# Weight slots at 0, 128 and 256 bytes modulo 512, and activation groups each at its own place, in a two-block transformer kernel

## The chip, the cores and the metric

The kernel runs on one core of one Trainium2 chip. The metric is the device time of one execution in microseconds. Three executions of the kernel before took 3440.49, 3443.15 and 3453.31 us; their median is 3443.15 us. The profiled execution is a separate one.

## The reference, cut to what matters

The input is one sequence of 512 tokens with 1024 features, all in float32. Two layers of a first block come first, each with a SwiGLU feed-forward part (1024 to 2816 and back), a token mixer (an attention with compressed, selected and windowed branches, beside a latent attention) and a second SwiGLU part. A hybrid layer follows, with an mLSTM, a forgetting attention, a gated linear recurrence, a gated linear attention, and a feed-forward part of 4096.

```python
for l in range(DEPTH):                       # DEPTH = 2
    mod = c_act @ w_ada[l] + b_ada[l]
    x = x + 0.5 * g1 * swiglu(modulate(x, sh1, sc1), ffn1_gate[l], ffn1_up[l], ffn1_down[l])
    x = x + g2 * token_mix(modulate(x, sh2, sc2), ...)
    x = x + 0.5 * g3 * swiglu(modulate(x, sh3, sc3), ffn2_gate[l], ffn2_up[l], ffn2_down[l])
x = rms_norm(x) * final_norm
...
z = h @ w_in + b_in                          # second block
merged = jnp.sum(g * yb, axis=2)
x = x + merged @ w_o
x = x + jnp.square(jax.nn.relu(h2 @ w_up)) @ w_down
```

Nearly all of the arithmetic is in products of an activation matrix with a weight matrix. The rest is small.

## The kernel before, in words

Activations stay in SBUF with features on the partitions, as tiles of 128 partitions by 512 tokens. Weights stream from HBM in a fixed order, written out by `plan()`: each step of it is one block of up to 1024 float32 per partition, loaded by SyncE into one of five `raw` buffers.

**Products in three parts.** Each large product is computed from operands that are split into a high and a low part, both in the type float32r. A weight block is split by ScalarE (line 971: `wh` is the rounded copy of `raw`) and VectorE (line 1492: `wl = raw - wh`), two steps of the plan ahead of TensorE. There are three slots (`NW = 3`), so `wh0` to `wh2` and `wl0` to `wl2`, used in turn by the split blocks. An activation is split in the same way into pairs such as `uh` and `ul`. TensorE then runs three matmuls for each 128 by 128 piece of weights (`three`, lines 451 to 453), with the weights as the stationary operand and the 512 tokens as the moving one:

```python
TE.matmul(o, w_hi(i, k), h, start=first, stop=False)
TE.matmul(o, w_lo(i, k), h, start=False, stop=False)
return TE.matmul(o, w_hi(i, k), l, start=False, stop=last)
```

`fm` (a whole product column), `fm_pair` (two of them interleaved) and the gate pieces during attention call it. Lines 538 to 540 are the same three for the first weights of the kernel. In `tm` (lines 485 to 487) the activations are stationary, in pieces of 128 tokens, and the weights move: 512 columns wide, or 280 wide for `inT` (three pieces of 280 columns in one slot, so they begin 0, 1120 and 2240 bytes after its start).

**Other matmuls** are plain float32: scores (673), transposes (568), attention times values (690, 696), sums over partitions (494, 512, 516), rows of norms (501), and filler matmuls (506).

**Order.** Each engine's program is written out by hand, and semaphores alone order the engines among each other. No wait hangs on where a tile lies. Addresses come from the order in which the tiles are declared: `sb()` puts each behind the one before it, at a multiple of 32 bytes, and tiles declared in a `with` block give their room to the next block.

**Places before.** All places here are bytes of one partition, modulo 512. The first tile, `cst`, begins at 128 and is 4764 bytes long, so `x` begins at 288; every tile between it and `mod` is a multiple of 512 bytes long. So `x`, `raw`, all `wh` and `wl`, `uh`, `ul`, `acc` and `tmp` begin at 288. The tiles `level` (64 bytes, after `mod` and `small`) and `level_mix` (384 bytes) hold no data and bring what follows to 288 again: `fh`, `fl`, `oA`, `oB`, `mq`, `mk`, `kk`, `vt`, `qh`, `ql`, `ch`, `cl`, `mP`, `mT`, `slope`, `oAh`, `oAl`, `oBh`, `oBl`, `merged`, `bh`, `bl` and `sg`. Exceptions are `mmask` and `mv` (416), `pcT` and `vc` (160), and the tiles of the second block's branches (`lqk` 416, `lE` 480). Pieces of a weight block follow each other in steps of 512 bytes, and the activation pieces in steps of 2048 bytes. So every float32r matmul but those 280 wide begins both of its reads at the same place modulo 512. The tables `ones`, `ident` and `sel` in `cst` are at 284.

Of the kernel before, what the change touches and what calls it, by code (L numbers as in the profile page):

```python
# [5 lines left out]
NW = 3  # L6
# [238 lines left out]
def program(nc, A, OUT):  # L245
# [3 lines left out]
    F32, F32R = mybir.dt.float32, mybir.dt.float32r  # L249
# [13 lines left out]
    top = ExitStack()  # L263

    def sb(ctx, name, shape, dt=F32):
        return ctx.enter_context(nc.sbuf_tensor(f"s_{name}", shape, dt))
# [2 lines left out]
    cst = sb(top, "cst", [128, ncol])  # L269
    x = sb(top, "x", [128, 8, 512])  # L270
    raw = [sb(top, f"raw{i}", [128, 1024]) for i in range(NRAW)]
    wh = [sb(top, f"wh{i}", [128, 1024], F32R) for i in range(NW)]
    wl = [sb(top, f"wl{i}", [128, 1024], F32R) for i in range(NW)]
    uh = sb(top, "uh", [128, 8, 512], F32R)
    ul = sb(top, "ul", [128, 8, 512], F32R)
    acc = sb(top, "acc", [128, 512])
# [3 lines left out]
    sb(top, "level", [128, 16])  # L280

    with ExitStack() as c:
        fh = sb(c, "fh", [128, CHUNK_FF, 512], F32R)
        fl = sb(c, "fl", [128, CHUNK_FF, 512], F32R)
        crow = sb(c, "crow", [128, 1024])
        more = sb(c, "more", [128, 512])
    with ExitStack() as c:
        fsq = sb(c, "fsq", [128, 8, 512])
    with ExitStack() as c:
        oA, oB = sb(c, "oA", [128, 4, 512]), sb(c, "oB", [128, 4, 512])  # L290
        mq = sb(c, "mq", [128, 8, 512])
        mk = sb(c, "mk", [128, 8, 512])
        with ExitStack() as c1:
            kk = sb(c1, "kk", [128, 2, 512])
            vt = sb(c1, "vt", [128, 4, 256])
            gt = sb(c1, "gt", [128, 4, 24])
            pcT = sb(c1, "pcT", [128, 4, 2, 128])
            vc = sb(c1, "vc", [128, 4, 128])
            kc = sb(c1, "kc", [128, 64])
            mmask = sb(c1, "mmask", [128, 512])  # L300
            mv = sb(c1, "mv", [128, 4, 512])
            sb(c1, "level_mix", [128, 96])
            with ExitStack() as c2:
                qh, ql = sb(c2, "qh", [128, 3, 512], F32R), sb(c2, "ql", [128, 3, 512], F32R)
                ch, cl = sb(c2, "ch", [128, 2, 512], F32R), sb(c2, "cl", [128, 2, 512], F32R)
            with ExitStack() as c2:
                dist = sb(c2, "dist", [128, 512])
                slope = [sb(c2, f"slope{i}", [128, 512]) for i in range(2)] + [tmp[2], tmp[3]]
                mP = [sb(c2, f"mP{i}", [128, 512]) for i in range(4)] + [tmp[0], tmp[1]]
                mT = [sb(c2, f"mT{i}", [128, 512]) for i in range(3)] + [acc]  # L310
                mfew = sb(c2, "mfew", [128, 24])
        oAh, oAl = sb(c, "oAh", [128, 4, 512], F32R), sb(c, "oAl", [128, 4, 512], F32R)
        oBh, oBl = sb(c, "oBh", [128, 4, 512], F32R), sb(c, "oBl", [128, 4, 512], F32R)
    with ExitStack() as c:
        merged = sb(c, "merged", [128, 8, 512])
        bh, bl = sb(c, "bh", [128, 4, 512], F32R), sb(c, "bl", [128, 4, 512], F32R)
        sg = sb(c, "sg", [128, 8, 512])
        bgh = sb(c, "bgh", [128, 32])
        ffx = sb(c, "ffx", [128, 512])
        rows = sb(c, "rows", [128, 512])  # L320
        with ExitStack() as d:
            lqk = sb(d, "lqk", [128, 8, 512])
            lmo = sb(d, "lmo", [128, 4, 512])
            lai, lmx = (sb(d, n, [4, 512]) for n in ("lai", "lmx"))
            lfm = sb(d, "lfm", [36, 512])[32:36, :]
            lsum = sb(d, "lsum", [128, 384])
            lcol = sb(d, "lcol", [128, 4, 4])
            lv = sb(d, "lv", [128, 4, 512])
            lE = [sb(d, f"lE{i}", [128, 512]) for i in range(4)]
        with ExitStack() as d:  # L330
            xqk = sb(d, "xqk", [128, 8, 512])
            xcol = sb(d, "xcol", [128, 4, 4])
            xgs = sb(d, "xgs", [128, 1])
            xsq = sb(d, "xsq", [128, 8, 512])
            xv = sb(d, "xv", [128, 4, 512])
            xP = [ffx] + [sb(d, f"xP{i}", [128, 512]) for i in range(3)]
            xT = [xsq[:, 5 + i, :] for i in range(3)]
            xfew = sb(d, "xfew", [128, 24])
        with ExitStack() as d:
            rbd = sb(d, "rbd", [128, 1024])  # L340
            rsp, rs1 = sb(d, "rsp", [128, 4]), sb(d, "rs1", [128, 4])
            rhb = sb(d, "rhb", [128, 12])
            rxc = sb(d, "rxc", [128, 4, 512])
            rR, rI, rT = (sb(d, n, [128, 4, 512]) for n in ("rR", "rI", "rT"))
            rgy = sb(d, "rgy", [128, 4, 512])
        with ExitStack() as d:
            gqk = sb(d, "gqk", [128, 4, 512])
            ggg = sb(d, "ggg", [128, 4, 512])
            ghs = sb(d, "ghs", [128, 4, 512])
            gE = sb(d, "gE", [128, 2, 512])  # L350
            gdec = sb(d, "gdec", [128, 2, 8])
            gv = sb(d, "gv", [128, 4, 512])
            gmask = sb(d, "gmask", [128, 512])
            gst = sb(d, "gst", [128, 2, 8, 128])
# [2155 lines left out]
```

## Time and profile before

| what | value |
|---|---|
| median of three executions | 3443.15 us |
| profiled execution, its own time | 3446.24 us |
| its span, first to last instruction | 3444.5 us |
| TensorE busy | 3401.3 us, 99% |
| VectorE busy | 1751.6 us, 51% |
| ScalarE busy | 1197.3 us, 35% |
| GpSimd busy | 262.0 us, 8% |
| granted TensorE clock, mean | 0.993 of full speed |
| DMA | 376.36 MB, mean 109 GB/s |

The span is the time between the first and the last recorded instruction; 1.7 us of the execution lie outside it. A group of the profile is one line of the kernel on one engine with its operands, the count, the union of its durations and the mean duration. A matmul's recorded duration is that from its start until its modelled end, and the next one starts before that end; so the pace of matmuls is read from their starts.

### The profile page before, as it was taken

The numbers are of one execution on the slowest core, as the hardware profiler recorded it, in microseconds if no ns is written. First come the engines' busy times: TensorE is split into PE (matmuls) and PEld (weight loads), VectorE is DVE, ScalarE is ACT, GpSimd is POOL, SyncE is SP. The second block draws the span as 40 slices with busy tenths as digits, with TensorE's granted clock in tenths as the row PEclk, the third lists the DMA queues.
The fourth block names the chain that finished last, engine by engine and source line by source line (L and its number), as shares of the span: only waits on it lengthen the run. The fifth ranks groups of instructions, "written<-read, shape, count | busy, mean of one in ns | idle before, by whom it ended". The sixth has DMA issues, their size and how long they took to land.

```text
span 3444.5 us, 40836 instructions
## 1 busy us (share of the span) xinstructions
PE 3401.3 (99%) x16686; PEld 2744.8 (80%) x16686; DVE 1751.6 (51%) x3014; ACT 1197.3 (35%) x2021; POOL 262.0 (8%) x219
## 2 busy tenths in 40 slices
PE   8999999999999999999999999999999999999999
PEld 7888886778888888887777888888778777878887
DVE  7666446565665733334655643334553555354433
ACT  3222336543222332223555332224322444233322
POOL 0000210002000200021100100013011000020000
PEclk9999999999999999999999999999999999999999
DMA  7565322123565533223210322323221223122332
GB/s 254 201 213 193 109 84 71 41 71 112 190 230 196 184 102 101 98 92 113 75 44 31 110 86 86 110 81 102 72 81 65 68 76 124 40 96 90 97 107 80
DMA packets 120361, 376.36 MB, mean 109 GB/s; under 512 B 13296, under 2 KB 28272, under 8 KB 120176
## 3 DMA queue, kind: packets, MB, share of 16 engines
q1 hardware_dynamic: 120176, 373.76, 32.9%
q8 instruction: 133, 2.18, 0.3%
q14 instruction: 52, 0.43, 0.0%
HBM read 371.61 MB, written 2.10 MB: 108 GB/s over the span
## 4 chain that ended last, share of the span: by engine, by line
PE 93%; DVE 4%; ACT 2%; issue 0%; DMA 0%; POOL 0%; SPq 0%; DVEq 0%; ACTq 0%; POOLq 0%
PE ps L451 26%; PE ps L453 26%; PE ps L452 26%; PE ps L673 2%; PE ps L696 2%; PE ps L568 2%; PE ps L485 1%; PE ps L486 1%; PE ps L487 1%; PE ps L501 1%; PE ps L494 1%; DVE s_wl L1492 1%; ACT s_wh L971 0%; PE ps L540 0%; PE ps L539 0%
## 5 line engine op out<-in xcount | busy, mean ns | idle before, releaser
L1492 DVE TENSOR_TENSOR s_wl<-s_raw,s_wh 128x1024 fp32r<-128x1024 f32 (+3 forms) x645 | 704.2, 1093 | 894.3 <-ACT s_wh L971 893.3
L451 PE MATMUL ps<-s_uh,s_wh 128*128 128x512 f32 x2824 | 1128.0, 399 | 10.0 <-DVE s_ul L1553 3.8
L453 PE MATMUL ps<-s_ul,s_wh 128*128 128x512 f32 x2824 | 1104.1, 391 | 0.4 <-issue 0.4
L452 PE MATMUL ps<-s_uh,s_wl 128*128 128x512 f32 x2824 | 1103.1, 391 | 0.0
L971 ACT ACTIVATE s_wh<-s_raw 128x1024 fp32r<-128x1024 f32 (+3 forms) x645 | 588.1, 914 | 706.9 <-PE ps L453 499.7
L451 PEld LDWEIGHTS ps<-s_uh,s_wh 128*128 128x128 f32 x2824 | 532.5, 189 | 152.7 <-issue 40.1
L453 PEld LDWEIGHTS ps<-s_ul,s_wh 128*128 128x128 f32 x2824 | 531.9, 188 | 113.7 <-issue 0.8
L452 PEld LDWEIGHTS ps<-s_uh,s_wl 128*128 128x128 f32 x2824 | 532.6, 189 | 107.6 <-issue 2.4
L451 PE MATMUL ps<-s_fh,s_wh 128*128 128x512 f32 x960 | 373.6, 389 | 0.2 <-DVE s_wl L1492 0.2
L452 PE MATMUL ps<-s_fh,s_wl 128*128 128x512 f32 x960 | 373.5, 389 | 0.0
L453 PE MATMUL ps<-s_fl,s_wh 128*128 128x512 f32 x960 | 373.5, 389 | 0.0
L1056 ACT ACTIVATE s_fh<-s_tmp 128x512 fp32r<-128x512 f32 x120 | 75.9, 632 | 407.2 <-DVE s_tmp L1602 382.4
L451 PEld LDWEIGHTS ps<-s_fh,s_wh 128*128 128x128 f32 x960 | 180.2, 188 | 37.9 <-issue 0.6
L453 PEld LDWEIGHTS ps<-s_fl,s_wh 128*128 128x128 f32 x960 | 180.2, 188 | 37.4
L452 PEld LDWEIGHTS ps<-s_fh,s_wl 128*128 128x128 f32 x960 | 180.2, 188 | 37.4
L1050 ACT ACTIVATE s_tmp<-ps 128x512 f32<-128x512 f32 x120 | 71.7, 598 | 342.4 <-PE ps L453 338.8
L1501 DVE CUSTOM_DVE_ANT_0 s_raw<-s_raw,s_crow 128x1024 f32<-128x1024 f32 x144 | 181.3, 1259 | 0.0
L1602 DVE TENSOR_TENSOR s_tmp<-s_tmp,ps 128x512 f32<-128x512 f32 x88 | 60.4, 687 | 170.1 <-PE ps L453 167.9
L2160 POOL TENSOR_TENSOR s_acc<-s_x 128x512 f32<-128x512 f32 x7 | 8.7, 1246 | 1600.7 <-DVE s_x L1584 1538.3
L1526 DVE TENSOR_TENSOR s_fl<-s_tmp,s_fh 128x512 fp32r<-128x512 f32 x120 | 83.1, 692 | 83.8 <-ACT s_fh L1056 83.8
L1176 ACT ACTIVATE s_mT<-ps 128x128 f32<-128x128 f32 (+3 forms) x144 | 57.2, 430 | 145.5 <-PE ps L568 145.5
L1584 DVE SCALAR_TENSOR_TENSOR s_x<-ps,s_mod,s_x 128x512 f32<-128x512 f32 (+1 forms) x86 | 60.7, 712 | 88.8 <-PE ps L453 88.5
(419 smaller groups left out, 3344.3 us busy)
## 6 DMA issues: line engine op xcount, KB each, us to landing
s_raw<-w SPq DMA_DIRECT2D x616, 512.0 KB, 3.6
s_raw<-w SPq DMA_DIRECT2D x96, 192.0 KB, 2.4
s_raw<-w SPq DMA_DIRECT2D x64, 256.0 KB, 2.6
s_raw<-w SPq DMA_DIRECT2D x19, 128.0 KB, 2.1
s_x<-x SPq DMA_DIRECT2D x4, 512.0 KB, 6.5
out<-s_x SPq DMA_DIRECT2D x8, 256.0 KB, 2.2
s_raw<-w SPq DMA_DIRECT2D x4, 420.0 KB, 4.2
s_crow<-crow SPq DMA_DIRECT2D x2, 512.0 KB, 5.9
```

Of the source, the lines that this page charges most:

```text
L451: TE.matmul(o, w_hi(i, k), h, start=first, stop=False)
L452: TE.matmul(o, w_lo(i, k), h, start=False, stop=False)
L453: return TE.matmul(o, w_hi(i, k), l, start=False, stop=last)
L568: ins = TE.transpose(o[:, sl(j)], p[:, sl(j)], ident)
L673: TE.matmul(o[g][:, 0:L], q, k, start=True, stop=True).then_inc(*s_pe.up(("ps", ("S", (st, 2 * t + g)))))
L696: ins = TE.matmul(o[g], v, mT[(n + g) % 4][:, sl(j)], start=kind == "mla" and j == 0, stop=j == i and (kind == "mla" or br == 1))
L971: SC.activation(wh[slot[t]][:, 0:n], raw[t % NRAW][:, 0:n], ACT.Copy).then_inc(*s_hi.up(("hi", t)))
L1050: SC.activation(s[:], bank(("g", st, jj))[:], ACT.Silu if u else ACT.Relu).then_inc(*s_act.up(("gate", st, jj), frees=("g", st, jj)))
L1056: SC.activation(fh[:, j, :], s[:], ACT.Copy).then_inc(*s_act.up(("hh", st, jj)))
L1492: V.tensor_tensor(wl[w][:, 0:n], raw[t % NRAW][:, 0:n], wh[w][:, 0:n].bitcast(F32), SUB).then_inc(*s_lo.up(("lo", t)))
L1501: V.tensor_tensor_reduce(raw[i % NRAW][:], raw[i % NRAW][:], crow[:], 1.0, 0.0, MUL, ADD, mod[:, o:o + 1]).then_inc(*s_dve.up(("raw", i)))
L1526: V.tensor_tensor(dst, src, hi.bitcast(F32), SUB).then_inc(*s_dve.up(key))
```

## The change

Tiles that hold no data are put between the others. The three pairs `wh` and `wl` are declared in turn, with a gap after each. `lai` and `lfm` become two ranges of partitions of one tile, which frees 2048 bytes. No instruction is added, removed or moved; the order of every engine stays.

```diff
-    wh = [sb(top, f"wh{i}", [128, 1024], F32R) for i in range(NW)]
-    wl = [sb(top, f"wl{i}", [128, 1024], F32R) for i in range(NW)]
+    sb(top, "gap0", [128, 56])
+    wh, wl = [], []
+    for i in range(NW):
+        wh.append(sb(top, f"wh{i}", [128, 1024], F32R))
+        wl.append(sb(top, f"wl{i}", [128, 1024], F32R))
+        sb(top, f"gap{i + 1}", [128, 64 if i == 2 else 32])
     uh = sb(top, "uh", [128, 8, 512], F32R)
...
     with ExitStack() as c:
+        sb(c, "gap_ffn", [128, 16])
         fh = sb(c, "fh", [128, CHUNK_FF, 512], F32R)
...
-            sb(c1, "level_mix", [128, 96])
+            sb(c1, "gap_mix", [128, 136])
...
+        sb(c, "gap_out", [128, 8])
         oAh, oAl = sb(c, "oAh", [128, 4, 512], F32R), sb(c, "oAl", [128, 4, 512], F32R)
...
         merged = sb(c, "merged", [128, 8, 512])
+        sb(c, "gap_branch", [128, 24])
         bh, bl = sb(c, "bh", [128, 4, 512], F32R), sb(c, "bl", [128, 4, 512], F32R)
...
-            lai, lmx = (sb(d, n, [4, 512]) for n in ("lai", "lmx"))
-            lfm = sb(d, "lfm", [36, 512])[32:36, :]
+            lmx = sb(d, "lmx", [4, 512])
+            laf = sb(d, "laf", [36, 512])
+            lai, lfm = laf[0:4, :], laf[32:36, :]
```

Places after, worked out from the sizes: slots of weights 0, 128 and 256; `uh`, `ul`, `acc`, `tmp`, `oA`, `oB`, `mq`, `mk`, `kk`, `vt` and `merged` 0; `fh`, `fl` 64; `qh`, `ql`, `ch`, `cl`, `mP`, `mT`, `slope` 160; `oAh` to `oBl` 32; `bh`, `bl`, `sg` 96; `pcT`, `vc` 384; `mmask`, `mv` 128. `cst`, `x` and `raw` stay at 128, 288 and 288.

The distance from the start of the stationary read to that of the moving one, in bytes modulo 512, was 0 for every pair of slot and activation, and becomes:

| activations | slot 0 | slot 1 | slot 2 |
|---|---|---|---|
| `uh`, `ul` (0) | 0 | 384 | 256 |
| `fh`, `fl` (64) | 64 | 448 | 320 |
| `bh`, `bl` (96) | 96 | 480 | 352 |
| `qh`, `ch` and their low parts (160) | 160 | 32 | 416 |
| `oAh`, `oBh` and their low parts (32) | 32 | 416 | 288 |

Where the weights move (lines 485 to 487) the signs are reversed.

## Rows read from the trace of the kernel before

**Rows 1.** The page, busy time: us, share of the span, instructions.
```profile
PE 3401.3 (99%) x16686; PEld 2744.8 (80%) x16686; DVE 1751.6 (51%) x3014; ACT 1197.3 (35%) x2021; POOL 262.0 (8%) x219
```

**Rows 2.** The page, the chain that ended last, shares of the span by engine.
```profile
PE 93%; DVE 4%; ACT 2%; issue 0%; DMA 0%; POOL 0%; SPq 0%; DVEq 0%; ACTq 0%; POOLq 0%
```

**Rows 3.** Groups by line and form, PE: count | busy us, mean ns | idle before.
```profile
L451 PE MATMUL ps<-s_uh,s_wh 128*128 128x512 f32 x2824 | 1128.0, 399 | 10.0 <-DVE s_ul L1553 3.8 <-DVE s_wl L1492 2.6 <-DVE s_ul L1862 1.8
L451 PE MATMUL ps<-s_fh,s_wh 128*128 128x512 f32 x960 | 373.6, 389 | 0.2 <-DVE s_wl L1492 0.2
...
L451 PE MATMUL ps<-s_bh,s_wh 128*128 128x512 f32 x128 | 50.3, 393 | 2.0 <-DVE s_wl L1492 1.2 <-DVE s_bl L1526 0.8
...
L485 PE MATMUL ps<-s_wh,s_uh 128*128 128x512 f32 x96 | 37.4, 389 | 0.0
...
L538 PE MATMUL ps<-s_uh,s_wh 128*128 128x512 f32 x64 | 25.1, 391 | 0.0
...
L451 PE MATMUL ps<-s_oBh,s_wh 128*128 128x512 f32 x64 | 24.9, 389 | 0.0
...
L451 PE MATMUL ps<-s_oAh,s_wh 128*128 128x512 f32 x64 | 24.9, 389 | 0.0
...
L485 PE MATMUL ps<-s_wh,s_uh 128*128 128x280 f32 x64 | 20.5, 320 | 0.0
...
L451 PE MATMUL ps<-s_qh,s_wh 128*128 128x512 f32 x48 | 19.3, 402 | 1.0 <-DVE s_wl L1492 1.0
...
L485 PE MATMUL ps<-s_wh,s_ch 128*128 128x512 f32 x16 | 6.4, 401 | 0.5 <-DVE s_wl L1492 0.5
...
L451 PE MATMUL ps<-s_ch,s_wh 128*128 128x512 f32 x16 | 6.2, 390 | 0.0
```

**Rows 4.** Lines 452 and 453 in steady stretches: duration ns min/median/max, first and last start us.
```profile
L452 PE MATMUL ps<-s_uh,s_wl x162: 388/389/390, 1200.1 to 1309.6; 128*128 128x512 f32 x162
...
L453 PE MATMUL ps<-s_fl,s_wh x68: 388/389/390, 1494.1 to 1539.7; 128*128 128x512 f32 x68
```

**Rows 5.** Timeline of PE behind a pause at 1997: start us, duration us.
```profile
1998.16 0.40 PE L452 MATMUL ps<-s_uh,s_wl 128*128 128x512 f32 x1
...
2000.24 0.39 PE L452 MATMUL ps<-s_uh,s_wl 128*128 128x512 f32 x1
```

**Rows 6.** Lines 452 and 453 from 560 to 720 us, in the first attention.
```profile
L452 PE MATMUL ps<-s_uh,s_wl x120: 387/393/402, 567.1 to 715.3; 128*128 128x512 f32 x120
...
L453 PE MATMUL ps<-s_ul,s_wh x120: 389/397/401, 567.3 to 715.5; 128*128 128x512 f32 x120
```

**Rows 7.** The 280-wide matmuls: two of the timeline, 20 starts apart, and durations from 482 to 488.
```profile
483.02 0.29 PE L485 MATMUL ps<-s_wh,s_uh 128*128 128x280 f32 x1
...
485.63 0.30 PE L487 MATMUL ps<-s_wl,s_uh 128*128 128x280 f32 x1
...
L486 PE MATMUL ps<-s_wh,s_ul x16: 287/297/298, 482.0 to 487.8; 128*128 128x280 f32 x16
...
L487 PE MATMUL ps<-s_wl,s_uh x17: 291/294/299, 481.7 to 488.0; 128*128 128x280 f32 x17
```

**Rows 8.** Plain float32 matmuls, lines 506 and 696: durations.
```profile
L506 PE MATMUL ps<-s_x,s_cst x56: 592/593/1201, 14.5 to 3091.3; 128*128 128x512 f32 x56
...
L696 PE MATMUL ps<-s_mT,s_vt x198: 272/273/323, 585.0 to 718.9; 128*64 128x128 f32 x198
L696 PE MATMUL ps<-s_mT,s_mv x94: 272/273/324, 539.7 to 580.7; 128*64 128x128 f32 x94
```

**Rows 9.** VectorE groups: line 1763 with two kinds of second operand, and line 1492.
```profile
L1763 DVE CUSTOM_DVE_ANT_0 s_mP<-ps,s_mmask 128x512 f32<-128x512 f32 x12 | 8.1, 686 | 3.8 <-PE ps L673 3.8
...
L1763 DVE CUSTOM_DVE_ANT_0 s_mP<-ps,s_slope 128x512 f32<-128x512 f32 x8 | 5.2, 687 | 4.6 <-PE ps L673 4.6
...
L1492 DVE TENSOR_TENSOR s_wl<-s_raw,s_wh 128x1024 fp32r<-128x1024 f32 x463 | 593.7, 1284 | 662.1 <-ACT s_wh L971 661.7
```

**Rows 10.** Who waited for whom, PE: us in total, times, longest us.
```profile
PE ps L451 <- DVE s_wl L1492: 5.0, 10, 1.2
```

## The prediction

> **What bounds the kernel now.** I read the page's busy times first. TensorE is busy for 3401.3 of 3444.5 us [rows 1], so idle time that a change could win back is 43 us at most. The chain of waits says the same: 93% of it is TensorE [rows 2]. The groups by form then show what TensorE does [rows 3]. The reader is to count there the float32r matmuls of 512 columns, and to multiply each row by three, since each of lines 451, 485 and 538 has two sisters with the same count. With `uh`: (2824 + 64 + 96) x 3 = 8952. With `fh`: 960 x 3 = 2880. With `bh`: 128 x 3 = 384. With `oAh` and `oBh`: 2 x 64 x 3 = 384. With `qh` 48 x 3 = 144, and with `ch` (16 + 16) x 3 = 96. In all 12,840. The 280-wide ones are 64 x 3 = 192 more.
>
> The durations of these rows (389 ns) overlap, so the pace comes from starts. In a steady stretch line 452 starts 162 times between 1200.1 and 1309.6 us, with two other matmuls between two of them: 109.5 / 161 / 3 = 0.2267 us [rows 4]. Streaming 512 columns at 2.4 GHz would be 213.3 ns, so each matmul pays 13.3 ns more. The second row there has the same duration of 389 ns with `fl` and `wh` [rows 4]: 45.6 / 67 / 3 = 0.2269 us. So 12,840 x 0.2267 = 2911 us, 85% of the span, are this one pace. It is what the change can touch: 1 ns on every matmul whose places change is worth their number in nanoseconds.
>
> **How many have their places changed.** Before, both reads of every 512-wide float32r matmul begin at the same place modulo 512. After, only `uh` and `ul` with slot 0 still do; the slots take turns, so that is a third of 8952, 2984. The other 12,840 - 2984 = 9856 get one of 14 new distances. So the price is 9.86 us for each nanosecond of mean pace.
>
> **What a nanosecond hangs on.** Duration and pace go together: 389 ns in the steady stretch stands for 226.7 ns, so a matmul's pace is its duration less 162 ns. Two places of the trace show paces other than 226.7.
>
> First, after each interruption the pace is unsteady for some ten matmuls. From 1998.16 to 2000.24 nine matmuls took 2.08 us, 231.1 ns each, then the pace falls to 226.7 and stays [rows 5]. In the first attention, where gate pieces run between transposes and scores and never more than a few in a row, the medians are 393 and 397 ns, so 231 and 235 ns; the lowest is 387 ns, the highest of these two rows 402 ns, so 225 and 240 ns [rows 6]. Nothing differs in these matmuls from those of the steady stretch but what ran before. So 226.7 ns isn't a fixed cost of a float32r matmul: it is a state into which the stream of moving reads and that of weight reads settle when both begin at the same place, and out of it the same instructions cost 4.4 ns more on the mean.
>
> Second, the 280-wide matmuls are the only float32r ones whose moving operand begins elsewhere: 0, 96 and 192 bytes past the stationary one. From 483.02 to 485.63 are 20 steps, 130.5 ns each, where 280 columns at 2.4 GHz and the same 13.3 ns would be 130.0. But they never settle: the durations run from 287 to 299 ns, so 125 to 137 ns, or -5 to +7 ns about that [rows 7]. So unequal places spread the pace, and on the mean cost 0.5 ns.
>
> **The sum.** The new distances aren't in the trace, but for 96 at another width, so the cost of a matmul whose places change is bounded: from below by the shortest 280-wide one, -5 ns (-49 us); from above by the median of line 453 in attention, 397 ns, +8 ns (+79 us). The two means are +0.5 ns [rows 7] and +4.4 ns [rows 5], +5 and +43 us. I take the middle of these, a mean of +2.2 ns: that is about half of the pairs staying unsettled at 231.1 ns, and half finding a settled pace as cheap as today's. 9856 x 2.2 ns = 21.7 us. TensorE is the chain, so all of it lands on the end.
>
> **The other parts, at nothing.** Plain float32 matmuls: line 506 takes 592 ns at a distance of 4 bytes and its operands stay. Line 696 takes a median of 273 ns both with `mT` and `vt` at the same place and with `mv` 128 bytes off [rows 8]. So their new places (`mP` and `mT` 160, `vt` 0) are taken at nothing, within 1 ns on some 1400 of them. VectorE and ScalarE: line 1763 takes 686 ns with a second operand 128 bytes off the output's place and 687 ns with one at the same place [rows 9]. Line 1492 will read `raw` at 288 and `wh` at 0, 128 or 256, at one place today. If that cost it a tenth of its 1284 ns, TensorE would still not see it: the split runs two steps ahead, a block of eight pieces lasts 24 x 0.2267 = 5.4 us, and TensorE waits for this line for 5.0 us in all today [rows 9, 10]. That wait is the bound: twice as much is +5 us. The packing of `lai` and `lfm` changes no instruction and adds no wait; DMAs go to `raw`, `x` and `cst`, which stay, and to a few tables once. Nothing new waits on SyncE's or GpSimd's queues.
>
> The sum stands against the profiled execution: 3446.24 + 21.7 = 3467.9 us. Its median neighbours are 3.1 us lower, so I forecast 3465 us.
>
> **A rule weighed.** TensorE's page of the Trainium skill ("TensorE: Matmul & The Clock Gate", "Step-by-step: what each phase is for") holds that the engine has two independent read ports: "Loading the next tile's weights doesn't steal SBUF read bandwidth from the running matmul." By that rule no place matters, the sum would be 0 and the time 3443 us. The trace only half agrees: the same instructions run at 225 to 240 ns [rows 6], though it can't show that the weight load is what they meet. The page's section "Back-to-back issue gap" gives N / 2.4 + 2.5 ns, 215.8 ns here, an estimate that this trace exceeds by 11 ns [rows 4].
>
> **Rivals.**
>
> *No effect.* The steady pace is the same for every slot and activation group [rows 4], as it must be when all are level; that says nothing on other distances. For it speaks the mean of the 280-wide ones, within 0.5 ns of level [rows 7], and that the stream settles by itself within ten matmuls after any interruption [rows 5]: it may do so from any distance. Against it, the 280-wide ones don't settle. It gives 0 to +5 us: 3443 to 3448 us.
>
> *Faster: the level start is itself the meeting that costs.* Both reads begin at the same place at the same moment, 12,840 times; apart, they might meet for less. The mechanism sits in each changed pair, and what speaks for it is 287 ns among the 280-wide ones, 5 ns under level, and 387 ns in attention, 2 ns under [rows 6, 7]. Against it: the mean there is no lower. At half of the 5 ns, 9856 x 2.5 = 25 us less, 3418 us. It decides over the forecast from the point where the mean of the 14 distances is below 226.7 ns, and passes 0.5% at -1.7 ns. If the whole 13.3 ns went, it would be -131 us, 3312 us; plain float32 shows that a stream with hardly any loss exists, but no float32r row comes near it.
>
> *Slower than forecast: none settles.* All 14 distances stay at 231.1 ns or above: 9856 x 4.4 = 43 us, 3486 us, and at the medians of line 453 3522 us. For it: the 280-wide ones never settle. This is the upper part of the forecast's own case.
>
> **How the numbers follow.** Mean pace higher (forecast and its upper part) 0.52; no effect 0.28; faster 0.20. About 0.5%, 17 us, is what a measurement of this kernel can tell from no change. Of the first case, which by itself reaches from 3450 to 3520 us, 0.06 lies under that bound; of the faster one 0.04. So slower 0.46, same 0.38, faster 0.16. The range leaves out 0.09 below (the stronger half of the faster case) and 0.1 above: 3424 to 3512 us.
>
> **What would show it.** In the profile after, with the same windows: line 451 to 453 with `uh` should fall into two kinds, blocks of 24 matmuls at 389 ns (slot 0) and blocks of others, up to 397 ns (slots 1 and 2). The 109.5 us that line 452 needs for 162 starts from 1200.1 us on [rows 4] should become some 110.2 (a third of them unchanged, the rest 2.2 ns longer). If a third of the blocks isn't still at 389 ns, distance isn't what matters. If lines 452 and 453 have 389 ns everywhere, the rival without effect is right. Medians under 389 ns for whole groups show the faster one. Line 1492's mean and TensorE's wait for it should stay at 1284 ns and about 5 us. The forecast is wrong altogether if the mean of plain float32 matmuls moves, or if TensorE's idle time does by over 5 us.

## The result and the profile after

| | before | after |
|---|---|---|
| median | 3443.15 us | 3493.16 us |
| lowest to highest | 3440.49 to 3453.31 | 3484.47 to 3497.65 |
| profiled execution, its own time | 3446.24 us | 3497.65 us |
| its span | 3444.5 us | 3495.9 us |
| granted TensorE clock, mean | 0.993 | 0.988 |

The changed kernel is slower: the ratio of the times is 1.0126, with a 95% interval of [1.0103, 1.0149] (the same stands behind every ratio below). A second measurement of it, beside other kernels (the eighth experiment), gave 1.0125 [1.0101, 1.0149]. The forecast was 3465 us with a range up to 3512 us: right in sign and range, 28 us too low. All lines of the changed kernel stand 8 lower in the file than before (451 is now 459, 1492 is 1500, 1763 is 1771).

The page after, first its busy times, then the shares of the chain that ended last:
```profile
PE 3454.5 (99%) x16686; PEld 2759.2 (79%) x16686; DVE 1754.8 (50%) x3014; ACT 1197.2 (34%) x2021; POOL 260.9 (7%) x219
PE 95%; DVE 3%; ACT 1%; issue 0%; DMA 0%; POOL 0%; SPq 0%; DVEq 0%; ACTq 0%; POOLq 0%
```
Every count is as it was [rows 1]. TensorE has 53.1 us more busy time, the span 51.4 us more, so TensorE's idle time fell by 1.7 us. The whole loss is in how long its instructions take.

The groups by form after, with count, busy time and mean duration of one:
```profile
L459 PE MATMUL ps<-s_uh,s_wh 128*128 128x512 f32 x2824 | 1137.5, 403 | 9.5 <-DVE s_ul L1561 3.8 <-DVE s_wl L1500 1.9 <-DVE s_ul L1870 1.8
...
L459 PE MATMUL ps<-s_fh,s_wh 128*128 128x512 f32 x960 | 377.6, 393 | 0.0
...
L459 PE MATMUL ps<-s_bh,s_wh 128*128 128x512 f32 x128 | 50.9, 398 | 1.6 <-DVE s_bl L1534 0.8 <-DVE s_wl L1500 0.8
...
L459 PE MATMUL ps<-s_oAh,s_wh 128*128 128x512 f32 x64 | 25.3, 395 | 0.0
...
L493 PE MATMUL ps<-s_wh,s_uh 128*128 128x280 f32 x64 | 20.5, 320 | 0.0
```
Set beside [rows 3], each 512-wide float32r group takes 4 to 6 ns more; the 280-wide one is unchanged at 320 ns.

The steady stretches of [rows 4] and the attention of [rows 6] after, with shortest, median and longest duration:
```profile
L460 PE MATMUL ps<-s_uh,s_wl x153: 387/389/404, 1205.3 to 1309.8; 128*128 128x512 f32 x153
L461 PE MATMUL ps<-s_fl,s_wh x46: 392/394/398, 1508.6 to 1539.9; 128*128 128x512 f32 x46
L460 PE MATMUL ps<-s_uh,s_wl x120: 387/393/402, 570.9 to 719.3; 128*128 128x512 f32 x120
L461 PE MATMUL ps<-s_ul,s_wh x120: 388/397/404, 571.1 to 719.5; 128*128 128x512 f32 x120
L704 PE MATMUL ps<-s_mT,s_vt x198: 272/273/323, 588.8 to 722.9; 128*64 128x128 f32 x198
L514 PE MATMUL ps<-s_x,s_cst x50: 592/592/1061, 387.0 to 3137.2; 128*128 128x512 f32 x50
```
Line 460 no longer has one duration: it was 388 to 390 ns, and is 387 to 404 ns. Line 461 with `fl` has not a single matmul left at 389 ns. In attention, where the pace was unsettled before, the medians are the same 393 and 397 ns: there was nothing to lose there. Plain float32 matmuls keep their 273 and 592 ns [rows 8].

**One border between two slots.** The timeline of TensorE, with start and duration in us. A block on slot 0 (distance 0) began at 1238.18; one on slot 1 (distance 384) runs from 1243.62 to 1249.21, then comes slot 2 (distance 256):
```profile
1238.18 0.39 PE L459 MATMUL ps<-s_uh,s_wh 128*128 128x512 f32 x1
...
1243.17 0.39 PE L460 MATMUL ps<-s_uh,s_wl 128*128 128x512 f32 x1
1243.39 0.40 PE L461 MATMUL ps<-s_ul,s_wh 128*128 128x512 f32 x1
1243.62 0.40 PE L459 MATMUL ps<-s_uh,s_wh 128*128 128x512 f32 x1
...
1249.21 0.39 PE L459 MATMUL ps<-s_uh,s_wh 128*128 128x512 f32 x1
...
1254.67 0.39 PE L459 MATMUL ps<-s_uh,s_wh 128*128 128x512 f32 x1
```
Each block has 24 matmuls: 5.44 us on slot 0 (226.7 ns each), 5.59 us on slot 1 (232.9 ns), 5.46 us on slot 2 (227.5 ns). The dear stretch seems to begin one matmul early. The one at 1243.39 still reads slot 0's weights at distance 0, but it has 0.40 us already, and the weights loaded while it streams are slot 1's. One row of 0.40 us is weak evidence by itself, since 0.39 and 0.40 also follow each other in an unsettled stream; the fourth experiment takes up the question.

**Mean pace by distance.** From the starts of all 512-wide float32r matmuls that follow another within one stream at full clock, sorted by slot and activation (mean ns from start to start, worked out from the trace, good to some 0.5 ns; in brackets the distance):

| activations | before (0) | slot 0 | slot 1 | slot 2 |
|---|---|---|---|---|
| `uh`, `ul` | 227.2 | 227.3 (0) | 232.6 (384) | 227.6 (256) |
| `fh`, `fl` | 226.7 | 230.2 (64) | 233.2 (448) | 229.9 (320) |
| `bh`, `bl` | 226.7 to 227.1 | 233.4 (96) | 233.1 (480) | 233.3 (352) |
| `oAh`, `oBh` | 226.7 | 233.5 (32) | 233.5 (416) | 233.4 (288) |
| `qh`, `ql` | 226.7 to 229 | 234.2 (160) | 233.3 (32) | 233.5 (416) |

Only 0 and 256 keep the settled pace. 64 and 320, which are 256 apart, cost 3 to 4 ns; all others 5.4 to 7 ns.

**The sum, and what it leaves.** The 9856 changed matmuls cost some 36.7 us by this table: 2984 x 0.4 ns with `uh` on slot 2, and the other 6872 at 5.1 ns on the mean. The span grew by 51.4 us. Setting the two traces beside each other instruction by instruction shows where the rest is: the lag is 28.6 us when before's trace is at 2944.6 us and 43.7 us at 2993.8 us, so 15.1 us came up in 49 us. The windows there (length, then busy time of PE, PEld, DVE, ACT, POOL with counts, granted clock, DMA share, GB/s), before first:
```profile
2960.00:2980.00 20.00, 20.00 (x110) 16.54 (x108) 3.18 (x3) 2.83 (x4) 4.04 (x4) 0.91 0.05 14
2980.00:3000.00 20.00, 20.00 (x106) 17.21 (x106) 10.53 (x27) 4.38 (x7) 3.94 (x4) 0.91 0.09 26
```
and after, some 29 us later in its own time:
```profile
2980.00:3000.00 20.00, 20.00 (x77) 16.15 (x77) 2.61 (x3) 2.72 (x4) 0.00 (x0) 0.54 0.04 13
3000.00:3020.00 20.00, 20.00 (x66) 15.92 (x66) 2.56 (x2) 2.83 (x4) 4.03 (x4) 0.52 0.00 1
```
TensorE is busy throughout in both, but after it has a granted clock of 0.54 and 0.52 for 40 us, that is its lower level of 1.2 GHz for nearly all of it, where before had 0.91. It starts 143 matmuls there against 216. The lower level holds without a break for 37.5 us:
```profile
2981.50:3019.00 37.50, 37.50 (x130) 30.12 (x127) 4.42 (x5) 5.54 (x8) 4.03 (x4) 0.50 0.02 7
```
So the profiled loss of 51 us is about 37 us of pace and 14 to 15 us of a longer stretch at half clock. In the lower-level stretch the timeline shows no pace loss at all:
```profile
3014.36 0.63 PE L460 MATMUL ps<-s_uh,s_wl 128*128 128x512 f32 x1
...
3018.20 0.63 PE L460 MATMUL ps<-s_uh,s_wl 128*128 128x512 f32 x1
```
Nine steps take 3.84 us, 426.7 ns each, just 512 columns at 1.2 GHz.

**The same split without a profile.** Each execution has a mean granted clock, and the time follows it in every kernel. The kernel before was run 43 times beside the experiments: at a clock of 0.993 it took 3444.75 to 3448.55 us (nine executions, median 3447.49), at 0.991 some 3453 us, at 0.990 some 3457 us, so some 3 us for each 0.001. One execution of the changed kernel had 0.993 too and took 3484.47 us, 37 us more; one at 0.992 (3486.78 us) is some 37 us above the three of before at 0.992 (3449.52 to 3450.26). So 37 us is what the changed kernel costs at the same clock, and the table above accounts for it. The rest of the ratio is a lower clock: 0.988 to 0.993, mean 0.9901, in the eight executions of the changed kernel here and in the eighth experiment, and 0.990 to 0.996, mean 0.9925, in the 43 of before. At 3 us for 0.001 the difference of the means is some 7 us.

### The profile page after: what moved, and what is told of

It reads as the page before. It is cut to its first block, busy times and chain, and to the rows that moved or that the text cites. A ratio compares the mean times of both kernels' runs of the same rounds, so it can differ in the third digit from the quotient of the medians.

```text
span 3495.9 us, 40836 instructions
## 1 busy us (share of the span) xinstructions
PE 3454.5 (99%) x16686; PEld 2759.2 (79%) x16686; DVE 1754.8 (50%) x3014; ACT 1197.2 (34%) x2021; POOL 260.9 (7%) x219
## 4 chain that ended last, share of the span: by engine, by line
PE 95%; DVE 3%; ACT 1%; issue 0%; DMA 0%; POOL 0%; SPq 0%; DVEq 0%; ACTq 0%; POOLq 0%
PE ps L459 27%; PE ps L461 26%; PE ps L460 26%; PE ps L681 2%; PE ps L704 2%; PE ps L576 2%; PE ps L493 1%; PE ps L494 1%; PE ps L495 1%; PE ps L509 1%; PE ps L502 1%; DVE s_wl L1500 0%; PE ps L546 0%; PE ps L548 0%; PE ps L547 0%; PE ps L913 0%
```

## The experiments

The first to fourth, sixth and seventh kernels differ from the one before in places alone, and keep the changed kernel's packing of `lai` and `lfm`. The fifth, ninth, eleventh and twelfth are edits of the kernel before, with its level places (both reads at the same place modulo 512); the eighth and tenth have the places of the change. A time "beside" is the median of the kernel before on the same chip. Diffs are cut to what matters. Steady stretches are taken as in [rows 4].

**First: is 256 bytes away the same as level?** All three slots at 256, all activations at 0.
```diff
+    sb(top, "gapw0", [128, 64])
     (wh0, wl0, wh1, wl1, wh2, wl2, with nothing between them)
+    sb(top, "gapw1", [128, 64])
```


> All three slots of weights lie at 256 modulo 512 and every activation group at 0, so every float32r pair of 512 columns has the distance 256. Theory A (places count modulo 256: the slot with distance 256 was as cheap after the change as the level one, 227.6 against 227.3 ns): pace 226.7 ns in steady stretches everywhere, time as before, 3443 us within 0.5%. Theory B (places count modulo 512, and slot 2 was cheap only because its blocks stand next to blocks of the level slot): the pace leaves 226.7 ns, by 4 ns or more on 12,840 matmuls, over 3490 us.

Measured: 3447.47 us beside 3447.86, ratio 0.9995 [0.9981, 1.001].
```profile
L461 PE MATMUL ps<-s_uh,s_wl x162: 389/389/389, 1200.2 to 1309.7; 128*128 128x512 f32 x162
L462 PE MATMUL ps<-s_fl,s_wh x59: 389/389/389, 1500.3 to 1539.7; 128*128 128x512 f32 x59
```
162 starts at 389 ns in 109.5 us, as in [rows 4]. Every float32r matmul changed its distance from 0 to 256, and nothing was lost. So a distance of 256 costs nothing, and the gaps and the packing cost nothing either.

**Second: the slots alone.** Slots at 0, 128 and 256, all activations at 0 (the four gaps ahead of activation groups of the change are left out).

> Only the slots are moved (0, 128, 256 modulo 512), all activation groups stay level at 0. Theory A: slots 0 and 2 at about 227 ns, slot 1 at about 232.6 ns for every activation group; 4280 matmuls x 6 ns = +26 us, 3469 us. Theory B (the number of places in use counts, not the distance): slot 2 is dear too in the feed-forward down products, +50 us or more. Rival that the weights' places do nothing by themselves: 3443 us.

Measured: 3477.27 us beside 3447.86, ratio 1.0085 [1.0054, 1.0116]; the profiled span is 28.4 us longer, at a mean clock of 0.993.
```profile
L462 PE MATMUL ps<-s_uh,s_wl x152: 387/389/404, 1205.6 to 1309.4; 128*128 128x512 f32 x152
L461 PE MATMUL ps<-s_fh,s_wh x47: 387/389/404, 1507.9 to 1539.6; 128*128 128x512 f32 x47
```
By slot the mean paces are 226.7 to 227.6, 232.7 to 233.3, and 227.6 to 229.5 ns. Slot 1 holds a third of the 12,840 matmuls, so 4280 x 5.7 = 24 us; the little of slot 2, highest in the short streams, is most of what is left.

**Third: the activations alone.** All slots at 0, activation groups where the change has them.

> Only the activation groups are moved (64, 160, 32, 96), all slots stay at 0, uh and ul too. Theory A: uh at 226.7 ns with every slot; fh (distance 64) at 230 ns as with slot 0 after the change, 2880 x 3.5 = 10 us; the others (32, 96, 160) at 233.4 ns, 1056 x 6.7 = 7 us: +17 us, 3460 us. Rival (it is the slots that matter, or moved tiles slow other engines): within 5 us of before.

Measured: 3463.78 us beside 3447.86, ratio 1.0046 [1.0028, 1.0063]; the profiled execution had 3454.6 us, the shortest of its ten, and a span 8.3 us longer than before.
```profile
L462 PE MATMUL ps<-s_uh,s_wl x163: 389/389/389, 1199.8 to 1309.9; 128*128 128x512 f32 x163
...
L461 PE MATMUL ps<-s_fh,s_wh x59: 394/394/394, 1500.1 to 1540.0; 128*128 128x512 f32 x59
L462 PE MATMUL ps<-s_fh,s_wl x59: 388/388/388, 1499.7 to 1539.5; 128*128 128x512 f32 x59
L463 PE MATMUL ps<-s_fl,s_wh x59: 392/392/392, 1499.9 to 1539.7; 128*128 128x512 f32 x59
```
`uh` is untouched. With `fh` at distance 64 the stream does settle, in another cycle: 394, 388, 392 ns for the three of a piece, 391.3 on the mean and 229 ns from start to start. Every other distance of this kernel (32, 96, 160) has 232 to 234 ns. The two halves of the change add up: 0.85% + 0.46% = 1.31%, against 1.26 and 1.25% for both together. They do so at equal clock as well: at 0.993 the slots alone took 3474.70 and 3475.18 us, 27 to 28 us over the 3447.49 of before, the activations alone 3458.18, 11 us over it, and both together 37 us. The ten executions of this third kernel had clocks of 0.988 to 0.994 and times up to 3475.24 us, and that, not the pace, is why its median is 5 us above the 3458 us.

**Fourth: which reads meet?** High parts of the weights at 0, low parts at 128, activations at 0. Of the three matmuls of a piece the second alone has its own weights at distance 128 (384 by the direction of the table above); and only during the first are such weights being loaded for the next.
```diff
+    wh.append(sb(top, "wh0", [128, 1024], F32R))
+    sb(top, "gapw0", [128, 32])
+    wl.append(sb(top, "wl0", [128, 1024], F32R))
+    sb(top, "gapw1", [128, 96])
```


> The high parts of the weights lie at 0 like all activations, the low parts at 128. Of the three matmuls of a piece, the second alone has weights 128 bytes off. Theory N (a matmul's moving reads meet the load of the NEXT matmul's weights, which runs at the same time): the first of the three (next weights: low part) loses time against 226.7 ns, the second, whose next weights are the high part, does not, or only by what is carried on. Theory O (a matmul's moving reads and its own weights): the second loses, the first does not. Sum of the three: between 680 + 6 ns (one of them dear) and 680 + 18 ns (never settled); 3470 to 3520 us.

Measured once: 3492.18 us beside 3447.86. The first, second and third of a piece take 396, 397 and 389 ns:
```profile
L464 PE MATMUL ps<-s_uh,s_wh x145: 396/396/474, 1210.1 to 1310.0; 128*128 128x512 f32 x145
L465 PE MATMUL ps<-s_uh,s_wl x144: 397/397/398, 1210.4 to 1309.5; 128*128 128x512 f32 x144
L466 PE MATMUL ps<-s_ul,s_wh x144: 389/389/389, 1210.6 to 1309.7; 128*128 128x512 f32 x144
```
From start to start these are 232.5, 234.1 and 226.7 ns. Neither simple answer holds. A matmul is not dear by its own weights alone, since the first is dear with its own at distance 0; nor by the next load alone, since the second is dear while a load at distance 0 goes on. The first's cost speaks for the load of the next weights, as the border above does; then the second must carry over what the first left behind. That is an inference. Two things in the weight loads' own records bear on it. Set beside the matmuls' starts, a load starts some 3 ns after the matmul ahead of it, so it does run beside that matmul's stream. And the load beside the dear second matmul, of weights at distance 0, takes 192 ns, where the same line's loads in the kernel before take 187 to 188 ns: it is held up too, though nothing is off in its own place.
```profile
L466 PEld LDWEIGHTS ps<-s_ul,s_wh x144: 189/192/192, 1210.4 to 1309.5; 128*128 128x128 f32 x144
L453 PEld LDWEIGHTS ps<-s_ul,s_wh x162: 187/188/188, 1200.1 to 1309.6; 128*128 128x128 f32 x162
```

**Fifth: does half of a load cost half?** The kernel before, with the second of three matmuls taking only 64 of its 128 weight columns; this leaves out the low part's product for rows 64 to 127 of each piece.
```diff
-            TE.matmul(o, w_lo(i, k), h, start=False, stop=False)
+            TE.matmul(o[0:64], w_lo(i, k)[:, 0:64], h, start=False, stop=False)
```


> Level places as before. The second of each three matmuls takes only 64 of the low part's 128 columns of weights (the low product of rows 64 to 127 is left out), so the load of these weights reads half as much. Theory N (the 13.3 ns over 512 columns are lost by moving reads to the load of the next matmul's weights): the first of the three falls to about 220 ns, second and third stay at 226.7 ns; 4200 x 6.7 = 28 us faster. Theory O (own weights): the second falls. Theory F (13.3 ns are a fixed cost of a float32r matmul): all stay at 226.7 ns, time as before.

Measured once: 3478.36 us beside 3444.75, 34 us more.
```profile
L451 PE MATMUL ps<-s_uh,s_wh x154: 388/389/472, 1204.0 to 1309.6; 128*128 128x512 f32 x154
L452 PE MATMUL ps<-s_uh,s_wl x154: 387/393/398, 1204.3 to 1309.8; 128*64 128x512 f32 x154
L453 PE MATMUL ps<-s_ul,s_wh x153: 387/393/398, 1204.6 to 1309.3; 128*128 128x512 f32 x153
```
Less to load made it slower: all places are level, yet the three have 228.8, 230.7 and 230.1 ns and never settle. So the 13.3 ns over pure streaming is not a price in proportion to the weights read, and level places are not enough for the settled pace. Whether it is the unlike loads or the shorter one that unsettles it, this kernel can't tell; the ninth takes that up.

**Sixth: every matmul at distance 160** (352 for the 336 of them in which the weights move). It sizes the full cost.
```diff
+    sb(top, "gapw0", [128, 88])
     (wh0, wl0, wh1, wl1, wh2, wl2, with nothing between them)
+    sb(top, "gapw1", [128, 40])
```


> All slots at 352 modulo 512, all activations at 0: every pair of 512 columns has the distance 160, the dearest of those seen after the change (234 ns). If cost goes by distance alone, 12,840 x 7 = 90 us more than before, 3530 us, and no matmul in a steady stretch at 389 ns of duration. If it were changes of distance between blocks that cost (each slot another), one distance for all would settle to 226.7 ns and the time stays at 3443 us.

Measured: 3530.68 us beside 3444.75, ratio 1.0253 [1.0227, 1.0278]; the span is 83.3 us longer.
```profile
L461 PE MATMUL ps<-s_uh,s_wl x125: 392/397/400, 1222.8 to 1309.9; 128*128 128x512 f32 x125
L462 PE MATMUL ps<-s_fl,s_wh x22: 392/397/400, 1200.0 to 1214.8; 128*128 128x512 f32 x22
```
The pace is 234.2 ns on the mean, in every group. Times 12,840, against the 227.2 ns with `uh` before, that is 90 us at most; 83 us show, since attention had unsettled matmuls already.

**Seventh: small distances.** Slots 0, 8 and 16 bytes off, `fh` and `fl` 4 bytes off.
```diff
+    for i, off in enumerate((0, 2, 4)):
+        both = sb(top, f"w{i}", [128, 2048 + (8 if off else 0)], F32R)
+        wh.append(both[:, off:off + 1024])
+        wl.append(both[:, off + 1024:off + 2048])
```


> Distances under 32 bytes: slots at 0, 8 and 16 modulo 512, uh, ul and the small groups at 0, fh and fl at 4, so distances 0, -8 and -16 with uh, and 4, -4 and -12 with fh. If reads meet in lines of 16 or 32 bytes, -8 and 4 behave like 0 or like a neighbour (226.7 or 233 ns) and nothing is under 226.7 ns. If the cost goes smoothly with distance, 4 and -4 are within 1 ns of 226.7 ns, perhaps under it. A pace under 226.7 ns for a group would point to a faster kernel: 1 ns on all is 13 us.

Measured once: 3506.17 us beside 3444.75.
```profile
L460 PE MATMUL ps<-s_uh,s_w x140: 389/392/397, 1213.2 to 1309.4; 128*128 128x512 f32 x140
L460 PE MATMUL ps<-s_fh,s_w x30: 395/400/404, 1519.2 to 1539.8; 128*128 128x512 f32 x30
```
Here the weights begin 8 or 16 bytes behind `uh`. With `uh` the slots have 227.4 (0 bytes), 231.0 (8 bytes) and 233.1 ns (16 bytes); with `fh`, at distances of 4 and 12 bytes, all have 236.8 to 237.1 ns, the dearest mean pace of any run here. No distance in any of these runs was cheaper than 226.7 ns.

**Eighth: the changed kernel again**, unedited, to see whether the long stretch at half clock was one execution's.

> The changed kernel unchanged, to see whether its profile keeps the stretch at half clock near 2985 to 3019 us. By the pace of its pairs the change is worth 37 us (3484 us profiled, beside 3446); the first profile had 14 us more from a longer stretch at half clock. Theory C (where the clock falls differs from execution to execution): this profile's granted clock is about 0.993 again and its time 3483 to 3488 us. Rival (the change itself prolongs the stretch at half clock): clock 0.988 again, over 3495 us.

Measured: 3492.85 us beside 3451.99, ratio 1.0125 [1.0101, 1.0149]; profiled 3494.3 us, mean clock 0.989.
```profile
2980.00:3000.00 20.00, 20.00 (x100) 16.38 (x100) 2.61 (x3) 2.77 (x5) 0.00 (x0) 0.71 0.05 14
3000.00:3020.00 20.00, 20.00 (x74) 16.17 (x72) 2.56 (x2) 2.77 (x4) 4.03 (x4) 0.61 0.05 14
```
The stretch comes back, 27.3 us long instead of 37.5, with all paces within 0.3 ns of the first profile:
```profile
2988.50:3015.80 27.30, 27.30 (x93) 21.92 (x92) 2.63 (x3) 3.42 (x5) 4.03 (x4) 0.50 0.01 2
```
So it was not a matter of one execution alone. But it isn't in every execution of this kernel either, as far as the mean clock tells: the four here had 0.989, 0.990, 0.989 and 0.992, the four of the result 0.988, 0.991, 0.993 and 0.989, and at 0.993 there is no room for a long stretch beside the short ones that before has.

**Ninth: half of all loads.** The kernel before with 64 of 128 weight columns in every matmul but those of a column's first and last piece; it leaves out rows 64 to 127 of the products between.
```diff
+            r = slice(0, 128 if first or last else 64)
+            TE.matmul(o[r], w_hi(i, k)[:, r], h, start=first, stop=False)
+            TE.matmul(o[r], w_lo(i, k)[:, r], h, start=False, stop=False)
+            return TE.matmul(o[r], w_hi(i, k)[:, r], l, start=False, stop=last)
```


> Level places. In every product column the matmuls of all pieces but the first and the last take only 64 of 128 columns of weights (rows 64 to 127 of these pieces are left out), so that most loads of weights read 256 bytes instead of 512, without the change of width at every third matmul. Theory N (13.3 ns are lost in proportion to what the load of weights reads): the middle 18 of 24 matmuls fall to about 220 ns, 60 us faster. Theory F (the pace follows from when the streams begin, not from how much the load reads): they do not fall under 226.7 ns, and may be over it, since the settled state is lost.

Measured once: 3478.68 us beside 3451.99. Three lines of the timeline, 12 steps from the first to the last:
```profile
1253.16 0.39 PE L452 MATMUL ps<-s_uh,s_wh 128*64 128x512 f32 x1
...
1254.54 0.39 PE L452 MATMUL ps<-s_uh,s_wh 128*64 128x512 f32 x1
...
1255.92 0.39 PE L452 MATMUL ps<-s_uh,s_wh 128*64 128x512 f32 x1
```
2.76 / 12 = 230.0 ns. The six of a cycle have 236, 229, 224, 227, 234 and 230 ns, again and again. Half the load is not cheaper even where nearly all loads are alike, and of the two widths tried level places settle at 226.7 ns with loads of 128 columns alone.

**Tenth and eleventh: does the stage's time decide?** 30 more filler matmuls ahead of the second block in the changed kernel, and 67 in the one before. I had priced a filler at 429 ns; it took 857, since each shows as two records of some 429 ns, so the shifts were 25.7 and 57.4 us.
```diff
-        keep_warm(spare, 1)
+        keep_warm(spare, 31)
```


> The changed kernel with 30 more filler matmuls (line 506's kind, 429 ns each, 12.9 us) ahead of the hybrid layer. Theory T (how long the gated linear attention runs at half clock depends on when it comes, not on the places): the stretch at half clock, 17 and 25 long float32r matmuls around 3004 to 3025 us in two profiles, shortens; clock 0.993, time 3493 + 13 - 10 = about 3496 us. Rival P (the places prolong it): the long stretch stays, clock 0.989, 3506 us.

Measured: 3512.65 us beside 3447.59, ratio 1.0195 [1.0136, 1.0255], the middle of two executions of 3519.85 us (profiled, clock 0.989) and 3505.45 us (clock 0.994). In the profile the stage of the long stretch has a granted clock of 0.79 over 80 us (table below): it stays there. The second execution, at 0.994, can't have had it. Less the 25.7 us of fillers that one took 3479.8 us, 36 us above the 3444 us that before took at 0.994: the cost of the pace once more.

> The kernel before with 67 more fillers there (28.7 us), which brings the gated linear attention to the same time as in the changed kernel, with level places. Theory T: the long stretch at half clock appears here, clock about 0.989, time 3446 + 29 + 12 = about 3487 us. Rival P: clock 0.993, 3475 us.

Measured: 3503.99 us beside 3447.59, span 3502.2, of which 57.4 us are fillers; the rest is 3444.8 us, the span of before. No long stretch. But the shift was twice the one meant, so this pair does not compare the two kernels at the same time. A second execution of the eleventh kernel took 4312.27 us at a mean granted clock of 0.749; it has no profile, and nothing here rests on it.

**Twelfth: the kernel before, shifted by what the change costs there.** 33 more fillers, 28.3 us, against the lag of 28.6 us.

> The fillers turned out to take 857 ns each, two passes of 429 ns, so the kernel before was moved by 57 us and not by 29. Here it has 33 more, 28.3 us, which brings the gated linear attention to the time that it has in the changed kernel, with level places. Theory T (time alone decides on the long stretch at half clock): over 15 long float32r matmuls in one stretch near 3000 us, clock about 0.989, 3446 + 28 + 10 = 3484 us. Rival P (the places matter to it): clock 0.993, 3474 us, as the kernel moved by 57 us kept 0.993.

Measured: 3475.12 us beside 3451.72, ratio 1.0076 [1.0058, 1.0094]; span 3474.2 us, which less 28.3 is 3445.9.
```profile
3000.00:3020.00 20.00, 20.00 (x106) 17.17 (x105) 6.66 (x20) 3.87 (x5) 7.97 (x8) 0.83 0.09 27
```
The same stage at the same time has a granted clock of 0.83 where the changed kernel has 0.52. So in this profile the delay alone does not bring the long stretch, and the four executions of the twelfth kernel, at 0.991 to 0.994, have no lower clocks than the kernel before unshifted. That leaves the places, something that the pace does before the stage, or a chance that differs from kernel to kernel; which, stays open. The mean granted clock over 80 us of this stage in each kernel's profile (from 2945 us on in before, and later in the others by what each had lost or been shifted until then):

| kernel | granted clock over 80 us |
|---|---|
| before; shifted by 57.4 and by 28.3 us | 0.96; 0.96, 0.96 |
| all 256 away; slots alone; activations alone; all at 160 | 0.96; 0.98; 0.96; 0.94 |
| low parts at 128; half a load in the second | 0.94; 0.94 |
| small distances | 0.89 |
| changed; changed again; changed and shifted | 0.74; 0.81; 0.79 |
| half of all loads (level) | 0.81 |

At 0.96 some 3 of the 80 us are lost, at 0.74 some 21. All three profiles with the changed kernel's places have the long stretch, and those of the two halves don't. But a profile is one execution: that of the activations alone was the shortest of its ten, and five of the ten had a mean clock of 0.988 to 0.990, as low as the changed kernel's. Where they lost it isn't on record. And a kernel with level places, the ninth, has the stretch in its one profile:
```profile
2968.00:2995.30 27.30, 27.30 (x102) 20.62 (x101) 3.30 (x4) 3.32 (x5) 0.00 (x0) 0.50 0.03 10
```
So the stretch isn't a property of the change. What is shown is that it comes in some executions and not in others, by the profiles and the mean clocks more often with the changed places than with those of before. No rule that I can state covers all of these.

## Why the prediction was right or wrong

**The bound and the count: right.** TensorE stayed the chain, idle time moved by 1.7 us, counts are the same. The plain float32 matmuls, VectorE and the other parts priced at nothing held: 273 and 592 ns again, line 1500 at 1289 ns against 1284, and TensorE waits less for it than before [rows 10]:
```profile
PE ps L459 <- DVE s_wl L1500: 3.3, 5, 1.2
```

**The mechanism: right in kind.** The prediction took 226.7 ns for a state into which two streams of reads settle when they begin at the same place, out of which the same matmuls cost more. The blocks did fall into two kinds, with slot 0 unchanged. It had "the same place modulo 512" from the fact that all were so; the first experiment shows that modulo 256 is enough. That both have to begin at the same place isn't the whole of it: the fifth and ninth experiments have level places and don't settle.

**The step that failed is the size of the mean, +2.2 ns.** It was called the middle of +0.5 and +4.4 ns, which is 2.45 ns (24 us, so some 3467 us); 2.2 ns is half of 4.4. That slip is 2 us and not what matters. It was also put as "about half of the pairs staying unsettled at 231.1 ns, and half finding a settled pace as cheap as today's". Of the 9856, only the 2984 at distance 256 settled so, 30% of them. (Counted matmul by matmul, 2904 keep their place and 2976 come to 256, since the blocks do not fall on the slots in equal parts; that moves the sum by under 1 us.) The rest sit at 229 to 234 ns, most of them above the 231.1 ns that [rows 5] gave for a stream on its way to settling. So the mean was +3.7 ns, 36.7 us instead of 21.7. The bounds (-5 and +8 ns) held: the dearest group of the change is at 234.2 ns. What misled was [rows 7]: the 280-wide matmuls at distances of 0, 96 and 192 had a mean within 0.5 ns of level, and they pulled the estimate down. At 512 columns the same distance of 96 costs 6.7 ns. The width was the difference between that row and the case, and the nearer one was [rows 6], at the right width: 231 and 235 ns, where most of the answer is.

**What was missing: the half clock.** No step of the prediction had a cost outside full clock. In the profile it is 14 to 15 us, half of the miss (3497.65 against 3467.9 us) and more than a quarter of the loss. The ratio of 1.0126 is 43 us, 37 of pace and some 6 of clock; the plain difference of the two medians, 50 us, starts from a median of few executions of before, 3443.15 us, which lies below most of the 43 later ones. Where the time goes in the profile and that it came again in two more are shown, its cause is not. The range held, but its upper part was priced by pace alone, so that a longer stretch at half clock fell inside it was luck.

**The named check.** "109.5 us should become some 110.2" was to be read from 162 starts of line 452. The page after gives 153 starts in 104.5 us (1205.3 to 1309.8): 687.5 ns a piece, so 110.7 us for 161 steps. The check told the sign and that the mean was above the forecast: 1.2 us more, not 0.7.

**The rivals.** *No effect* is refuted by the second, third and sixth experiments: nothing but places differs between the first experiment (226.7 ns) and the sixth (234.2 ns). That it is the places of weights and stream against each other is shown, since moving either alone costs time (second and third) and moving both to 256 apart does not. That the two meet while the next weights are loaded is argued from the fourth. The Trainium skill says under "TensorE: Matmul & The Clock Gate", in "Step-by-step: what each phase is for", that a load of the next weights steals no read bandwidth from the running matmul. These runs don't agree that the load's place has no effect on the running matmul; but a load half as large is no cheaper, so it need not be bandwidth that is lost. *Faster* is refuted: no distance tried, 4, 8 and 16 bytes among them, has a mean pace under 226.7 ns. *None settles* was put as the forecast's upper part at 3486 us, 43 us of pace; with 37 us measured it is nearer than the forecast's 21.7, though one distance of the change does settle.

## What to carry to other kernels

In a stream of 512-wide float32r matmuls, whose weights (128 columns) change with every matmul, declare both operands so that their starts are equal modulo 256 bytes: here it is worth up to 2.5% of the whole kernel and costs only padding. Read the pace from starts, and group them by the pair of buffers before taking a mean; a row that shares the distance but not the width is no substitute for one that shares the width. Before a difference of half a per cent is put down to an edit, compare the granted clock of the same stage in both traces, and compare executions of both kernels at the same mean clock: that alone gave the 37 us that took a table of paces to find.

## What the hardware did that was not expected

- The cost goes by the distance modulo 256 bytes: 0 and 256 settle at 226.7 ns; 64 and 320 have 229 to 230.5 ns; 32, 96, 128, 160, 192 and 224 (each modulo 256) have 232 to 234.2 ns; 4 and 12 bytes have 237, 8 bytes 231 and 16 bytes 233 ns. Of these, 0, 32, 64, 96 and 160 were also seen 256 bytes further on, with the same pace within 1.5 ns; 128, 192 and 224 were seen at one of the two alone.
- In the fourth experiment a matmul whose own weights are level takes 232.5 ns, while weights at another place are loaded for the next.
- Loading 64 weight columns in place of 128 raised the mean pace from 226.7 to 230.0 ns, at level places (fifth and ninth experiments).
- At 1.2 GHz the matmuls run at 426.7 ns, with nothing on top of 512 columns; at 2.4 GHz the best is 13.3 ns on top of 213.3.
- A plain float32 filler of 512 columns takes 857 ns and shows as two records.
- The same 80 us stage had a granted clock of 0.74 to 0.81 in all three profiles with the changed kernel's places, and 0.96 in the three of the kernel before, shifted or not; but 0.81 also in the ninth kernel, whose places are those of before. TensorE was busy all through.
- Executions of one and the same kernel differ in mean granted clock, 0.990 to 0.996 in 43 of the kernel before, and some 3 us of its time go with each 0.001.
